# Expert weights of a mixture of experts held as three whole slots instead of four half slots

## The reference, cut to what matters

```python
def moe_swiglu(h, router_w, w1, w3, w2):      # h: 256 x 1024; w1, w3: 8 x 1024 x 2816; w2: 8 x 2816 x 1024
    logits = xt @ router_w                    # 256 x 8
    top_val, top_idx = lax.top_k(logits, 2)
    gates = softmax(top_val)
    # for each expert e, over the tokens that chose it:
    y = (silu(x @ w1[e]) * (x @ w3[e])) @ w2[e]
    # out[token] = sum over its two experts of gate * y
```

## Time and profile before

| | us |
|---|---|
| median of 3 runs | 1949.4 |
| lowest and highest | 1948.94, 1952.83 |
| the profiled execution | 1949.06 |
| its span, first to last instruction | 1947.3 |

### The profile page before, as it was taken

How to read it: one execution, slowest core, us unless ns; L and a number is a source line. 1 busy time by engine, 2 the same in 40 slices (tenths; PEclk the granted TensorE clock), 3 DMA queues, 4 the chain that set the end, 5 groups by cost and what they waited for, 6 DMA issues and landing times.

```text
span 1947.3 us, 27157 instructions
## 1 busy us (share of the span) xinstructions
PE 1871.4 (96%) x10640; PEld 1618.8 (83%) x10640; DVE 1534.0 (79%) x2105; ACT 1195.7 (61%) x1642; POOL 50.4 (3%) x56
## 2 busy tenths in 40 slices
PE   7999999999999999999999999899899989999998
PEld 7889998777888888888888887698789978878997
DVE  5768887567999999999999998657589985756565
ACT  4444445635888888888888887557554446744443
POOL 0010000002000000000000010000000000000000
PEclk9999999999999999999999999999999999999999
DMA  7348886744999999999999999343278974324551
GB/s 313 130 158 307 327 345 256 283 170 151 423 387 382 388 372 387 379 384 376 387 376 386 368 407 376 120 152 111 85 262 337 356 269 149 114 82 178 181 194 44
DMA packets 75902, 528.39 MB, mean 271 GB/s; under 512 B 8659, under 2 KB 9043, under 8 KB 14323
## 3 DMA queue, kind: packets, MB, share of 16 engines
q1 hardware_dynamic: 69536, 504.40, 67.8%
q10 hardware_dynamic: 3060, 11.02, 1.6%
q0 software_dynamic: 3168, 11.14, 1.4%
HBM read 515.90 MB, written 11.01 MB: 271 GB/s over the span
## 4 chain that ended last, share of the span: by engine, by line
PE 89%; DVE 5%; ACT 3%; issue 1%; POOL 1%; DMA 0%; POOLq 0%; SPq 0%; ACTq 0%; DVEq 0%
PE ps L554 28%; PE ps L556 27%; PE ps L555 27%; PE ps L775 2%; DVE w_lo L1396 1%; PE ps L727 1%; ACT w_hi L2301 1%; PE ps L990 1%; PE ps L740 1%; POOL stat L2812 1%; DMA ring<-in_stream 0%; ACT xT L2311 0%; PE ps L818 0%; ACT score L2422 0%; PE ps L973 0%
## 5 line engine op out<-in xcount | busy, mean ns | idle before, releaser
L2301 ACT ACTIVATE w_hi<-ring 128x1024 fp32r<-128x1024 f32 x862 | 911.2, 1061 | 592.9 <-PE ps L556 587.5
L1396 DVE TENSOR_TENSOR w_lo<-ring,w_hi 128x1024 fp32r<-128x1024 f32 x862 | 1040.4, 1222 | 254.3 <-ACT w_hi L2301 242.9
L554 PE MATMUL ps<-w_hi,x_hi 128*128 128x512 f32 (+1 forms) x1056 | 410.8, 391 | 8.7 <-DVE w_lo L1396 3.6
L556 PE MATMUL ps<-w_hi,x_lo 128*128 128x512 f32 (+1 forms) x1056 | 400.2, 381 | 0.0
L555 PE MATMUL ps<-w_lo,x_hi 128*128 128x512 f32 (+1 forms) x1056 | 399.2, 380 | 0.0
L554 PE MATMUL ps<-x_hi,w_hi 128*128 128x256 f32 x1248 | 359.7, 288 | 5.7 <-DVE x_lo L1511 4.6
L555 PE MATMUL ps<-x_lo,w_hi 128*128 128x256 f32 x1248 | 355.1, 285 | 0.0
L556 PE MATMUL ps<-x_hi,w_lo 128*128 128x256 f32 x1248 | 354.9, 284 | 0.0
L554 PE MATMUL ps<-w_hi,h_hi 128*128 128x512 f32 x732 | 285.1, 390 | 0.9 <-DVE h_lo L2028 0.9
L555 PE MATMUL ps<-w_lo,h_hi 128*128 128x512 f32 x732 | 284.9, 389 | 0.0
L556 PE MATMUL ps<-w_hi,h_lo 128*128 128x512 f32 x732 | 284.3, 388 | 0.0
(11 more groups left out here) (298 smaller groups left out, 1306.8 us busy)
## 6 DMA issues: line engine op xcount, KB each, us to landing
ring<-in_stream SPq DMA_DIRECT2D x479, 1024.0 KB, 6.9
x_store<-arena ACTq DMA_DIRECT2D x1, 4096.0 KB, 28.9
arena<-x_store POOLq DMA_DIRECT2D x7, 512.0 KB, 8.4
y_store<-y_slots POOLq DMA_DIRECT2D x7, 512.0 KB, 8.7
con<-in_consts ACTq DMA_DIRECT2D x1, 2048.0 KB, 21.5
arena<-in_ln_rows ACTq DMA_DIRECT2D x3, 512.0 KB, 4.3
resid<-in_x SPq DMA_DIRECT2D x1, 1024.0 KB, 6.3
arena<-in_c ACTq DMA_DIRECT2D x2, 512.0 KB, 3.8
```

The lines of the kernel that those rows point to most:

```text
L554: pe.matmul(out_, lhs[0], rhs[0], start=start, stop=False)
L556: return pe.matmul(out_, lhs[1], rhs[0], start=False, stop=stop)
L1396: dve.tensor_tensor(lo, ring[:, q % RING, a:a + HALF], hi.bitcast(F32), ALU.subtract)\
L2301: act.activation(half_buffer(m)[0], ring[:, q % RING, a:a + HALF], ACT.Copy).then_inc(hi_ready, 1)
```

## The change

Outside the experts all buffers stay as they were. In the experts, a buffer holds a whole slot, and there are three: the first two halves of `w_hi` with the first two of `w_lo`; the place of the attention scores (high) with the place of `xT` (low); the third half of `w_hi` and of `w_lo` (high) with the first 2048 columns of `arena` (low). VectorE makes the low part of a slot in one operation of 2048 columns, when both high parts are there. ScalarE goes on making high parts by halves. `sel`, `selg` and `selT` move out of `arena` into `ff`. Places in the queues:

- ScalarE makes one more high part (half 135, the fourth) between the squares of the two row blocks; in a step the high parts stand partly ahead of `moe_hi` and partly ahead of Silu, by other bounds than before.
- VectorE makes slot 66's low part before the logits (before: one half in the branch addition, one after the first take), and slot 67's between the first selection and the first take.
- In a step VectorE makes the low part of slot n+3 between `moe_lo` and the gating product, and those of n+4 and n+5 behind the gating product, ahead of the selection, the merges and the take.

```diff
--- before.py
+++ after.py
@@ -36,7 +36,7 @@
 HALF = SLOT // 2
 RING = 6
 PAIRS = 3
-MOE_PAIRS = 4
+MOE_SLOTS = 3
 F1 = 2816
 NE = 8
 J1 = F1 // 256
@@ -119,11 +119,19 @@
 def buffers_of_halves():
 
     moe = range(2 * W_MOE, 2 * W_PLE1)
-    buffer = [(m - moe.start) % MOE_PAIRS if m in moe else m % PAIRS for m in range(2 * SLOTS)]
-    held, before = {}, []
-    for m, b in enumerate(buffer):
-        before.append(held.get(b, -1))
-        held[b] = m
+    buffer, held, before = [], {}, []
+    for m in range(2 * SLOTS):
+        if m in moe:
+            b, i = PAIRS + (m - moe.start) // 2 % MOE_SLOTS, m % 2
+            parts = {PAIRS: (i, PAIRS + i), PAIRS + 1: (("score", i), ("xT", i)),
+                     PAIRS + 2: (2 + PAIRS * i, ("arena", i))}[b]
+        else:
+            b = m % PAIRS
+            parts = (b, PAIRS + b)
+        buffer.append(b)
+        before.append(max(held.get(part, -1) for part in parts))
+        for part in parts:
+            held[part] = m
     return buffer, before
 
 
@@ -234,17 +242,21 @@
 
         ps = ctx.enter_context(nc.psum_tensor("ps", [P, 8, BANK], F32))
         ring = sb("ring", [P, RING, SLOT])
-        w_hi = sb("w_hi", [P, PAIRS, HALF], F32R)
-        w_lo = sb("w_lo", [P, PAIRS, HALF], F32R)
+        w_all = sb("w_all", [P, 2 * PAIRS, HALF], F32R)
+        w_hi, w_lo = w_all[:, 0:PAIRS, :], w_all[:, PAIRS:2 * PAIRS, :]
         x_hi = sb("x_hi", [P, KT, S], F32R)
         x_lo = sb("x_lo", [P, KT, S], F32R)
         h_hi = sb("h_hi", [P, 2, BANK], F32R)
         h_lo = sb("h_lo", [P, 2, BANK], F32R)
         resid = sb("resid", [P, QB, D])
+        xT_at = nc.sbuf_base
         xT = sb("xT", [P, KT, S])
+        assert nc.sbuf_base == xT_at + 4 * KT * S
         rows = sb("rows", [P, QB, D])
         ff = sb("ff", [P, 3, BANK])
+        arena_at = nc.sbuf_base
         arena = sb("arena", [P, 8192])
+        assert nc.sbuf_base == arena_at + 4 * 8192
         grow = sb("grow", [P, 2, D])
         con = sb("con", [P, NCOLS])
         ones = sb("ones", [P, P])
@@ -300,9 +312,9 @@
         ws = arena[:, 6144:7168].rearrange("p (g t) -> p g t", g=8)
         moe_gain = ln_b
 
-        sel = arena[:, 0:256].rearrange("p (b c) -> p b c", b=QB)
-        selg = arena[:, 256:512].rearrange("p (b c) -> p b c", b=QB)
-        selT = arena[:, 512:768].rearrange("p (b s) -> p b s", b=QB)
+        sel = ff[:, 0, 0:256].rearrange("p (b c) -> p b c", b=QB)
+        selg = ff[:, 0, 256:512].rearrange("p (b c) -> p b c", b=QB)
+        selT = ff[:, 1, 0:256].rearrange("p (b s) -> p b s", b=QB)
         y_rows = arena[:, 1024:2048]
         picked = arena[:, 3072:7168].rearrange("p (b c n) -> p b c n", b=QB, c=2)
         x_slots = arena[:, 7168:8192]
@@ -329,8 +341,9 @@
         score_at = (top_at - 4 * 2 * 4 * (S + 1)) // 64 * 64
         assert nc.sbuf_base <= score_at, (nc.sbuf_base, score_at)
         score = nc.alloc_sbuf_tensor_at("score", [P, 2, 4, S + 1], F32, offset=score_at)
-        w_hi3 = nc.alloc_sbuf_tensor_at("w_hi3", [P, HALF], F32R, offset=score_at)
-        w_lo3 = nc.alloc_sbuf_tensor_at("w_lo3", [P, HALF], F32R, offset=score_at + 4 * HALF)
+        w_score = nc.alloc_sbuf_tensor_at("w_score", [P, 2, HALF], F32R, offset=score_at)
+        w_xT = nc.alloc_sbuf_tensor_at("w_xT", [P, 2, HALF], F32R, offset=xT_at)
+        w_arena = nc.alloc_sbuf_tensor_at("w_arena", [P, 2, HALF], F32R, offset=arena_at)
         y_hi = nc.alloc_sbuf_tensor_at("y_hi", [P, D], F32R, offset=top_at)
         y_lo = nc.alloc_sbuf_tensor_at("y_lo", [P, D], F32R, offset=top_at + 4 * D)
         y_slots = nc.alloc_sbuf_tensor_at("y_slots", [P, D], F32, offset=top_at)
@@ -341,9 +354,15 @@
         scratch = xT[:, :, :].rearrange("p k s -> p (k s)")
         blk = scratch[:, 1024:1536].rearrange("p (v l n) -> p v l n", v=2, n=16)
 
+        moe_slots = ((w_all[:, 0:2, :], w_all[:, PAIRS:PAIRS + 2, :]),
+                     (w_score[:, :, :], w_xT[:, :, :]),
+                     (w_all[:, 2:2 * PAIRS:PAIRS, :], w_arena[:, :, :]))
+
         def half_buffer(m):
             b = BUFFER[m]
-            return (w_hi[:, b, :], w_lo[:, b, :]) if b < PAIRS else (w_hi3[:, :], w_lo3[:, :])
+            if b < PAIRS:
+                return w_hi[:, b, :], w_lo[:, b, :]
+            return tuple(v[:, m % 2, :] for v in moe_slots[b - PAIRS])
 
         def bank(b, n=1):
             return ps[:, b:b + n, :].rearrange("p b n -> p (b n)")
@@ -1389,10 +1408,18 @@
                     if m % 2 == 0:
                         for slot in ada_before(m // 2):
                             fold(slot)
+                    q = PLACE["work", m // 2]
+                    if BUFFER[m] >= PAIRS:
+                        if m % 2 == 0 and m + 2 <= m_end:
+                            dve.wait_ge(hi_ready, m + 2)
+                            hi, lo = moe_slots[BUFFER[m] - PAIRS]
+                            whole = ring[:, q % RING, :].rearrange("p (a n) -> p a n", a=2)
+                            dve.tensor_tensor(lo, whole, hi.bitcast(F32), ALU.subtract).then_inc(lo_ready, 2)
+                            split_at[0] = m + 2
+                        continue
                     dve.wait_ge(hi_ready, m + 1)
                     a = m % 2 * HALF
                     hi, lo = half_buffer(m)
-                    q = PLACE["work", m // 2]
                     dve.tensor_tensor(lo, ring[:, q % RING, a:a + HALF], hi.bitcast(F32), ALU.subtract)\
                         .then_inc(lo_ready, 1)
                     split_at[0] = m + 1
@@ -1938,6 +1965,7 @@
                     split_to(reach(u0 + 7))
             add_branch(4, W_COUT + 4, first_half=1)
             norm(4, gain(4))
+            split_to(2 * W_MOE + 2)
             dve.wait_ge(logits_ready, 1)
             link(dve.tensor_copy(logit[:, :, :].rearrange("p b e -> p (b e)"), ps[:, 0, 0:16]))
             for t in range(QB):
@@ -2049,14 +2077,14 @@
                 e, j = s // J1, s % J1
                 n = up_slot(s)
                 if s >= 1:
-                    split_to(reach(2 * n + 1))
                     moe_lo(s - 1)
-                    split_to(reach(2 * (n + 1)))
-                split_to(reach(2 * (n + 2)))
+                split_to(2 * n + 8)
                 dve.wait_ge(moe.act_ready, s + 1)
                 dve.tensor_tensor(hid_rows[:, s % 2, :], act_rows[:, s % 2, :], ps[:, s % 2, 256:512], ALU.mult)                    .then_inc(moe.hid_ready, 1)
                 if s == 0:
                     find_spots()
+                if s + 1 < STEPS:
+                    split_to(2 * up_slot(s + 1) + 6)
                 if e == NE - 1 and j == 2:
                     select(moe, e)
                 if e == NE - 1 and 5 <= j < 9:
@@ -2114,10 +2142,10 @@
                 dve.wait_ge(w.merged, e(1, 2))
 
             select(moe, 0)
+            split_to(2 * W_MOE + 4)
             take(moe, [1, 2])
             for s in range(STEPS):
                 moe_step(s)
-            split_to(reach(2 * down_slot(STEPS - 1)))
             moe_lo(STEPS - 1)
             split_to(2 * W_PLE1)
             split_end[0] = 2 * SLOTS
@@ -2577,7 +2605,7 @@
             act.dma_start(moe_gain, ln_rows[2].partition_broadcast(P)).then_inc(moe_gain_in, 16)
             keep_gated(1)
             split_to(2 * (W_COUT + 4) + 1)
-            square_rows(4, 2 * (W_COUT + 4) + PAIRS)
+            square_rows(4, 2 * (W_COUT + 4) + 4)
             act.wait_ge(route_asked, 1)
             for t in range(QB):
                 act.activation(route[:, t, 1, 1:2], route[:, t, 1, 0:1], ACT.Exp).then_inc(route_exp, 1)
@@ -2611,9 +2639,10 @@
                 if j == 1 and e >= 1:
                     keep_y(e - 1)
                 if s >= 1:
-                    split_to(reach(2 * (n + 1)))
+                    split_to(reach(2 * n + 1))
                     moe_hi(s - 1)
-                slots_done(n + 2)
+                split_to(reach(2 * n + 3))
+                act.wait_ge(half_done, 2 * (n + 2))
                 act.activation(act_rows[:, s % 2, :], ps[:, s % 2, 0:256], ACT.Silu).then_inc(moe.act_ready, 1)
                 if e == NE - 1 and j == 5:
                     act.wait_ge(moe.selT_ready, 1)
```

## The result

The changed kernel takes 1951.76 us, the median of 20 runs (1949.96 to 1956.38); the kernel before, run beside it, 1948.83 (1946.87 to 1952.9). The ratio is 1.0015, with a 95% interval of 1.0009 to 1.0022: 2.9 us slower, inside the 0.2% called the same. The prediction was 1951.3, with 1948.5 to 1955.5 as its range. The profiled execution of after is one of its slower ones: 1954.91 us, span 1953.1. Its span is 5.8 us longer than that of before's profiled execution (1947.3), not 2.9, so the two traces are compared stage by stage, and the rest is accounted for on its own.

A forecast was written before the change was run, and what follows sets the result against it. TensorE was taken to set each of 88 expert steps of 8.41 us. The terms 0.9 - 0.6 + 2.1 - 0.4 = +2.0 us on the profiled 1949.06 gave 1951.1, as median 1951.3, range 1948.5 to 1955.5.

The forecast's parts named there:

- Steady steps 0, loads 0: Expert stage: steps stay at TensorE's 8.42 us, and weights land in time, costing 0, up to +2.5 us.
- Rival 1: Expert steps: VectorE becomes the bound; at 2.55 us per operation each step is 0.1 longer, 1960 us; chance 0.04.
- rival 2: Around 500 us: scattered rows make slots land late, TensorE idles 2.5 us once, 1953.8 us; chance 0.13.
- rival 4: Expert products: TensorE's 0.227 us spacing shrinks by 3 ns for each of 3168 products, 1940 us; chance 0.03.
- The operation: VectorE's low part: 2048 columns take 2.29 us, the next starts after 2.20; 0.07 saved per slot, hidden behind TensorE.
- rival 5: Expert switches: they cost 0.65 us each, with VectorE operations that don't overlap, 1953.8 us; chance 0.06.
- Norm +0.9: Norm at the stage's entry: the fourth high part between ScalarE's squares delays what follows by 0.9 us.
- Low parts at the entry 0: Entry: whole low parts of slots 66 and 67 fit where VectorE idles, costing 0, the second with 0.5 to spare.
- First step -0.6: First expert step: TensorE's 0.64 us wait before the first turn goes, as Silu's table loads earlier; -0.6 us.
- Switches +0.3 each: Seven expert switches: VectorE's take delays the hidden rows' low part, TensorE waits 0.3 us each, +2.1 us in all.
- End -0.4: Last expert's steps with merges: VectorE's queue falls from 8.67 to 8.47 us, about 0.2 comes back twice.
- Rival 3: Expert switches: they cost nothing, as ScalarE and VectorE run 0.3 us ahead of the walk, 1949.2 us; chance 0.20.

The follow-up runs named there:

- control: The changed kernel with no edit, run again beside edited versions: 1952.22 us, ratio 1.0022 to the kernel before.
- e2: The changed kernel with the fourth high part made behind both squares, not between them: 1950.55 us, ratio 1.0006 to the kernel before.
- e1: The changed kernel with VectorE's take of the next expert's rows moved behind the hidden rows' low part: 1951.07 us, ratio 1.0013 to before.
- e3: The changed kernel with both edits, e1's moved take and e2's later fourth high part: 1946.02 us, ratio 0.9992 to the kernel before.
- e4: The changed kernel with each low part made in two 1024-column operations, each after its own high part: 1948.97 us, ratio 0.9998 to before.
- e9: The changed kernel with e4's two 1024-column operations and e2's later fourth high part: 1946.52 us, ratio 0.9989 to the kernel before.
- e7: The kernel before with only the fourth high part made between the squares: 1952.13 us, ratio 1.0013 to the kernel before.

## Why the prediction was right, and where not

The forecast was a sum of four terms, beside others put at nothing; here each stands against what the traces of after and of its control show.

- **Steady steps 0, loads 0.** Right: 8.41 to 8.44 in both kernels (and once in each of seven experts 9.3 in both), and no wait of TensorE for a landing. Rival 1 fell with the 2.29 us, rival 2 with the waits, rival 4 with TensorE's step, which is the same to 0.01. Rival 1 was priced too low: at 2.55 us three operations of a step would be 0.27 longer together, not 0.1, 24 us in all. Rival 4's 1940 leaves out the +2.
- **The operation.** Right: 2.29 us, starts 2.20 apart (540.38 and 542.58). The Trainium skill, VectorE: DVE Perf Modes, The DRAIN you can't avoid, would have had them 2.29 apart by its rule that the next operation doesn't start until the pipe is empty, from which the same section excepts one that is not held. The trace has the next one start 0.09 before the end of the last, so rival 5 had no ground.
- **Norm +0.9.** Right: 0.90 in every kernel with the part early, 0.00 in every one with it late. In the runs at equal clock it is 1.4 between control and e2, 1.0 between e1 and e3, 1.2 between e4 and e9, and 1.5 between e7 and before. What no term had is the clock: as measured the same operation costs 2.5 to 4.0.
- **Low parts at the entry 0.** Right, with 0.57 to spare where 0.5 was forecast.
- **First step -0.6.** The size was near: -0.8 to the first turn, and +0.16 in the step behind it (8.64 for 8.48), as the hidden rows' low part stands behind slot 70's. The reason named was partly wrong. "The high part of half 135 and the next two are done earlier": half 135 has no part in it, since e7 has it early and keeps the wait, and e2 has it late and loses it. What is left of the change is the third held slot and the order of ScalarE's queue; these two weren't parted.
- **Switches +0.3 each.** The walk was right and the price wrong. It had the down products start 3.29 behind the turn (545.2 - 541.91); they start 3.25 behind it (546.46 - 543.21), where the same step of before has 2.99 (544.90 - 541.91). So 0.26 of waiting, but the step is 0.43 longer. The missing 0.17 is the restart: the first product behind the wait lasts 0.50 and the next starts 0.34 after it, where in a stream it is 0.227. That is 0.11, and the rest is in the next eleven, which come 0.232 apart. It was to be seen in the trace of before, at the first expert product:

```profile
464.44 0.50 PE L554 MATMUL ps<-w_hi,x_hi 128*128 128x512 f32 x1 [1.41 <-DVE x_lo L1998]
...
464.78 0.40 PE L555 MATMUL ps<-w_lo,x_hi 128*128 128x512 f32 x1
```

Seven times it made 3.0 instead of 2.1.
- **End -0.4.** It was -0.7, and for another reason. The term went by the length of VectorE's queue, 8.67 and 8.47 (its addends for before make 8.65). e4 has before's length of queue and after's gain:

```profile
1191.41 2.35 DVE L1418 TENSOR_TENSOR w_arena<-ring,w_all 128x1024 fp32r<-128x1024 f32 x2
...
1200.08 2.35 DVE L1418 TENSOR_TENSOR w_arena<-ring,w_all 128x1024 fp32r<-128x1024 f32 x2
```

These are e4's rows of VectorE for the same slot in two successive steps with a merge, 8.67 apart, and its TensorE turns 8.43 and 8.41 apart all the same. So the length of VectorE's queue did not set these steps. It seems that VectorE can fall 0.25 behind in each of two steps as long as it has a lead to lose, and that e4 has it from the third held slot with its queue order; neither the lead nor what each part gives to it was measured.

The sum, from the traces: 0.9 - 0.8 + 0.16 + 3.0 - 0.7 = +2.55, and +2.66 +- 0.50 in the runs at equal clock, against +2.0 forecast. The switch term was 0.9 too small and the others 0.35 too large, so the sum is nearer than its largest term. As measured it is +2.9 in the medians of the first runs and +3.7 in the control's, which fits a cost of the clock on top that the forecast didn't have. That the time itself, 1951.3, came within 0.5 us of 1951.76 is luck in part: it was built on 1949.4, the median of 3 runs of before, and 20 runs gave 1948.83. Rival 3, that the switches cost nothing, had the highest chance of the rivals, and e1 shows what it would have been: 2.7 us less.

## What to carry to other kernels

One long operation in place of two saved 0.07 us of queue here, and delayed its own start until the last input was there and with it everything behind; it can pay where the engine bounds the time and nothing urgent stands behind it, and this engine didn't bound it. Where a bottleneck engine waits in a few places of an otherwise full stage, look for the item that is queued ahead of the one it needs, on both queues, and move that; and price the wait with the engine's restart, not by its length alone. Where the terms are 1 to 3 us and runs lie 9 us apart, compare at equal granted clock, and take the length of each stage from the traces; then compare the mean clocks themselves, for an operation placed where the bottleneck engine has little to do can cost more through the clock than through its length.

## What the runs showed of the hardware that was not expected

- A stream of 512-column products that is broken for 0.26 us loses 0.43: the first product behind the gap is 0.50 instead of 0.39 (546.46 above), and the next starts 0.34 behind it and not 0.227.
- The granted clock explains most of the spread between runs of one kernel: 1.38 us of span for each 0.001 of its mean, with 0.71 us left over.
- The mean granted clock is not the same for all kernels: 0.9871 over 90 runs with one high part made early in a norm, 0.9882 over 137 with it made late, and e7 and before, which differ in nothing else, have 0.9869 and 0.9881.
- TensorE is granted 1.2 GHz again in the middle of a kernel, behind short stretches of little work: 2.32 busy of 4 us was followed by 4 us at 0.57 in e2 and, in the kernel before, the same 2.32 of 4 by 4 us at 1.00, so like work has it in one execution and not in another. On the path, such a stretch took 1.6 us in the gathering (5.19 for 3.56).
